# Norms of q and kv and the key rotation moved into the input projection, the convolution norms' steps listed per engine, the dilated up map ahead of the sparse one

## The reference

```
z = modulate(rmsnorm(x, g_pre_mix), shift, scale) @ w_in      # 1024 -> 1696 columns
zq, ckv, k_rope, conf, sc = parts of z                        # 256, 128, 32, 512, 768
q = rmsnorm(zq, g_q) @ w_q_b; q's last 32 of 96 columns of a head are rotated
k, v = rmsnorm(ckv, g_kv) @ w_kv_b; k_rope is rotated, and shared by all 8 heads
attn = softmax(q k / sqrt(96)) v
conf = silu(layernorm(depthwise_conv(a * sigmoid(g), 31 taps)))
sc   = b * depthwise_conv(c * h, 3 taps)
y = concat(rmsnorm(attn), rmsnorm(conf), rmsnorm(sc)) @ w_o
x = x + gate * rmsnorm(y, g_post_mix); then the same around w2(relu(w1 h)^2)
```

```
merged = sigmoid(m0) * (y_nsa @ w_up_nsa) + sigmoid(m1) * (y_dil @ w_up_dil)
x = x + merged @ w_o;  x = x + peer(rms_norm(x))      # product-key experts
```

## Time and profile before

| what | us |
|---|---|
| median of 3 runs | 4206.3 (4204.83 to 4207.1) |
| profiled execution | 4206.12 |
| its span | 4204.8 |
| PE busy | 3946.2 (94%) |
| PEld busy | 3112.9 (74%) |
| DVE busy | 2139.9 (51%) |
| ACT busy | 1520.0 (36%) |
| POOL busy | 495.0 (12%) |

### The profile page before, as it was taken

One profiled execution on the slowest core, in us unless ns is written; L12 is line 12 of the kernel. 1 busy time (PEld: TensorE's weight loads), 2 busy tenths in 40 slices (PEclk: granted clock), 3 DMA queues, 4 the chain that ended last, 5 costly groups with the idle time before them and its releaser, 6 DMA issues.

```text
span 4204.8 us, 47670 instructions
## 1 busy us (share of the span) xinstructions
PE 3946.2 (94%) x19722; PEld 3112.9 (74%) x19722; DVE 2139.9 (51%) x3752; ACT 1520.0 (36%) x1876; POOL 495.0 (12%) x748
## 2 busy tenths in 40 slices
PE   6988989999898889998899989999998999999999
PEld 4845768888774468885787877878887788888887
DVE  2165343333446444444544445788873566654444
ACT  3245442212235542225554423344443322222222
POOL 0000000000000000000001000267556111100000
PEclk8999999999999999999999999999999999999999
DMA  5400122332110022222214232354545666543332
GB/s 189 164 18 1 61 78 104 120 111 100 51 70 13 1 80 90 90 100 95 74 38 127 82 119 92 137 169 156 169 153 186 189 193 187 180 150 116 110 126 85
DMA packets 109832, 459.76 MB, mean 109 GB/s; under 512 B 9216, under 2 KB 43120, under 8 KB 68912
## 3 DMA queue, kind: packets, MB, share of 16 engines
q1 hardware_dynamic: 82048, 354.96, 24.3%
q0 software_dynamic: 27568, 101.74, 8.1%
HBM read 389.04 MB, written 67.63 MB: 109 GB/s over the span
## 4 chain that ended last, share of the span: by engine, by line
PE 81%; DVE 8%; ACT 5%; POOL 2%; DMA 2%; issue 1%; SPq 0%; DVEq 0%; ACTq 0%; POOLq 0%
PE ps L554 22%; PE ps L556 22%; PE ps L555 22%; PE ps L2323 2%; PE ps L981 2%; PE ps L634 1%; DVE ACC L1194 1%; POOL Y L2459 1%; PE ps L476 1%; DVE MX L1167 1%; PE ps L1061 1%; PE ps L1870 1%; DVE TD L711 1%; DMA gdram<-GST 1%; PE ps L1889 1%
## 5 line engine op out<-in xcount | busy, mean ns | idle before, releaser
L554 PE MATMUL ps<-HH,WH 128*128 128x512 f32 x2760 | 1058.1, 383 | 54.1 <-DVE HL L675 36.5
L555 PE MATMUL ps<-HL,WH 128*128 128x512 f32 x2760 | 1048.8, 380 | 0.0
L556 PE MATMUL ps<-HH,WL 128*128 128x512 f32 x2760 | 1048.8, 380 | 0.0
L447 DVE TENSOR_TENSOR WL<-stage,WH 128x2048 fp32r<-128x2048 f32 x248 | 567.3, 2287 | 483.6 <-ACT WH L436 483.6
L436 ACT ACTIVATE WH<-stage 128x2048 fp32r<-128x2048 f32 x248 | 472.8, 1907 | 585.8 <-PE ps L556 539.6
L554 PEld LDWEIGHTS ps<-HH,WH 128*128 128x128 f32 x2760 | 523.7, 190 | 167.1 <-issue 51.0
L556 PEld LDWEIGHTS ps<-HH,WL 128*128 128x128 f32 x2760 | 524.8, 190 | 105.7
L555 PEld LDWEIGHTS ps<-HL,WH 128*128 128x128 f32 x2760 | 523.7, 190 | 102.6 <-issue 0.5
L554 PE MATMUL ps<-AHp,WH 128*128 128x512 f32 x1024 | 406.9, 397 | 7.1 <-ACT Y L2641 7.1
L555 PE MATMUL ps<-ALp,WH 128*128 128x512 f32 x1024 | 406.5, 397 | 0.0
L556 PE MATMUL ps<-AHp,WL 128*128 128x512 f32 x1024 | 406.4, 397 | 0.0
(11 more groups left out here) (366 smaller groups left out, 4955.3 us busy)
## 6 DMA issues: line engine op xcount, KB each, us to landing
stage<-in_w SPq DMA_DIRECT2D x64, 1024.0 KB, 4.8
stage<-in_u SPq DMA_DIRECT2D x64, 1024.0 KB, 4.9
stage<-in_v SPq DMA_DIRECT2D x64, 1024.0 KB, 4.9
stage<-in_w_mod SPq DMA_DIRECT2D x48, 1024.0 KB, 4.9
GR<-gdram POOLq DMA_DIRECT2D x32, 1024.0 KB, 7.9
adram<-GR SPq DMA_DIRECT2D x22, 1024.0 KB, 3.9
AR<-adram POOLq DMA_DIRECT2D x88, 256.0 KB, 3.5
gdram<-GST SPq DMA_DIRECT2D x16, 1024.0 KB, 5.8
```

The lines of the kernel that those rows point to most:

```text
L447: dve.e.tensor_tensor(k.WL[o % 2][:, 0:w], k.stage[n % 2][:, 0:w], k.WH[o % 2][:, 0:w].bitcast(F32), ALU.subtract).then_inc(*dve.done("sla ...
L554: pe.e.matmul(o, wh[:, kk, cs], L.hh[:, kk, z], start=first, stop=False)
L555: pe.e.matmul(o, wh[:, kk, cs], L.hl[:, kk, z], start=False, stop=False)
L556: mm = pe.e.matmul(o, wl[:, kk, cs], L.hh[:, kk, z], start=False, stop=last)
```

## The change

In w_in, ScalarE squares kv and q after chunk q1, into three rows of Y instead of TA (the ring ZS). After chunk g1 TensorE sums them, and ScalarE does both Ln and then both Exp. After chunk a1 TensorE rotates the key, and DVE scales kv and q and finishes the rope. WKV moves to the place of the TD buffers, outside of what w_in's inputs occupy, and is loaded as soon as the key is rotated; the ropes of q inside attention get scratch of their own (TDa). WQ's load stays where it was. V's six products and copies become entries of `att_order`, between the three parts of head 0.

`att_behind` names the sum ("stat"), the root, the scaling ("normed", "centered") and the SiLU as separate entries; both products of a sum stand together; the PSUM tile of a sum is held until the entry of its root; the taps of the short convolution are spread between them. The sums of a pair of heads go into Y's own rows.

In the merge the dilated map comes first, in the plan of slabs too, and the three DVE steps go to the sparse chunks. w_o2 waits for each low part by itself and pairs its first two chunks.

```diff
     k.ta = [new(f"TA{i}", [128, 768]) for i in range(2)]
+    k.WKV = nc.alloc_sbuf_tensor_at("WKV", [128, 1024], F32, offset=base.at)
     k.td = [new(f"TD{i}", [128, 768]) for i in range(2)]
...
     k.WQ = new("WQ", [128, 2, 768])
-    k.WKV = new("WKV", [128, 1024])
+    k.tda = [new(f"TDa{i}", [96, 512]) for i in range(2)]
...
         plain(("dvs", hp), 1, lambda s: io[f"dvs{hp}"])
     plain("wmg", 8, lambda s: io["wmg"][s])
+    plain("up_dil", 1, lambda s: io["up_dil"])
     plain("up_nsa", 2, lambda s: io["up_nsa"][s])
-    plain("up_dil", 1, lambda s: io["up_dil"])
     plain("w_o2", 4, lambda s: io["w_o2"][s])
     plain("wq2", 4, lambda s: io["wq2"][s])
     for g in range(32):
...
-def tensor_stat(k, pe, name, c, n, segs, ring=None):
-    ring = ring or k.psum
+def tensor_stat(k, pe, name, c, n, segs, ring=None, squares=None, keep=False):
+    ring, squares = ring or k.psum, squares or k.TA
     if c == 0:
...
 def tensor_z(k, pe, l):
+    segs = both(l)
     for c in tensor_linear(k, pe, z_linear(k, l)):
-        pass
+        if c == 6:
+            tensor_stat(k, pe, ("kvn", l), 0, 1, [LAT, CTX], None, k.ZS)
+            for j in range(2):
+                tensor_stat(k, pe, ("qn", l), j, 2, segs, None, k.ZS)
+        if c == 7:
+            p = k.psum.take(pe, ("krot", l), ("rope_s", (l, "k")))
+            pe.wait_ge("z_act", (l, "kr"))
+            pe.wait_ge("rotM", 0)
+            pe.e.matmul(p[0:96, 0:512], k.rotM[:, :], k.KR[:, 0:512], start=True, stop=True).then_inc(*pe.done("rot", (l, "k")))
 def scalar_z(k, act, l):
...
         i.then_inc(*act.done("z_act", (l, kind)))
+        if kind == "q1":
+            act.wait_ge("z_act", (l, "q1"))
+            scalar_square(k, act, ("kvn", l), 0, k.ZKV, 0, 768, k.ZS)
+            for j in range(2):
+                scalar_square(k, act, ("qn", l), j, k.ZQ[:, j, :], a, b, k.ZS)
+        if kind == "g1":
+            rows = [(("kvn", l), 128, [LAT, CTX], ("kv_normed", l)), (("qn", l), 256, both(l), ("q_normed", l))]
+            for name, D, segs, end in rows:
+                scalar_rstd_log(k, act, name, 1 if D == 128 else 2, D, segs, k.psum, end)
+            for name, D, segs, end in rows:
+                scalar_rstd_root(k, act, name, segs)
 def vector_z(k, dve, l):
...
         i.then_inc(*dve.done("z_dve", (l, kind)))
+        if kind == "a1":
+            col, segs = k.cols[l], both(l)
+            vector_norm_in_place(k, dve, ("kvn", l), [k.ZKV[:, :]], [LAT, CTX], lambda c: col[:, G_KV + c:G_KV + c + 1],
+                                 ("kv_normed", l))
+            vector_norm_in_place(k, dve, ("qn", l), [k.ZQ[:, j, :] for j in range(2)], segs,
+                                 lambda c: col[:, G_Q + c:G_Q + c + 1], ("q_normed", l))
+            vector_rope(k, dve, k.KR, ("krot", l), (l, "k"))
...
 def att_behind(l):
-    out = []
+    out, short = [], []
     for j in range(2):
         out += [("tap", 0, j, t) for t in range(31)] + [("conv", 4 + j)]
     for j in range(2):
-        out += [("tap", 1, j, t) for t in range(3)] + [("conv", 6 + j)]
-    out += [("center",), ("sq", "conf", 0), ("sq", "conf", 1), ("silu",)]
-    out += [("sq", "br4", 0), ("sq", "br4", 1), ("branch", 4)]
-    return out + [("sq", "br6", 0), ("sq", "br6", 1), ("branch", 6)]
+        short += [("tap", 1, j, t) for t in range(3)] + [("conv", 6 + j)]
+    out += [("center",)] + short[0:2] + [("centered",)] + short[2:4] + [("sq", "conf", 0), ("sq", "conf", 1)]
+    out += short[4:6] + [("stat", "conf")] + short[6:8] + [("root", "conf"), ("sq", "br6", 0), ("sq", "br6", 1)]
+    out += [("normed",), ("stat", "br6"), (None,), ("silu",), ("root", "br6"), ("sq", "br4", 0), ("sq", "br4", 1)]
+    return out + [("branch", 6), ("stat", "br4"), (None,), ("root", "br4"), (None,), ("branch", 4)]
 def att_order(l):
...
     scored, turned, outs, pairs, head, done = [], [], [], [], [], 0
-    for part in range(3):
-        yield "head", (0, part)
+    yield "head", (0, 0)
+    for tt in range(4):
+        yield "v", tt
+    yield "head", (0, 1)
+    yield "v", 4
+    yield "v", 5
+    yield "head", (0, 2)
     for n, u in enumerate(units + [None, None, None]):
         ended = pairs.pop(0) if pairs else None
         if outs:
...
 def tensor_att(k, pe, l):
     segs = both(l)
     if l == 0:
         tensor_mod_close(k, pe, 0, 21)
     for kind, u in att_order(l):
         if kind == "head":
             tensor_head(k, pe, l, *u)
+        elif kind == "v":
+            p = k.psum.take(pe, ("v", l, u), ("v", (l, u)))
+            pe.wait_ge("kv_normed", l)
+            pe.wait_ge(f"wkv{l}", 0)
+            pe.e.matmul(p[:, 0:512], k.ZKV[:, 128 * u:128 * u + 128],
+                        k.WKV[:, :].rearrange("p (h a d) -> p h a d", h=8, a=2)[:, :, 1, :],
+                        start=True, stop=True).then_inc(*pe.done("v_mm", (l, u)))
         elif kind == "scores":
             h, q0, k0, kn = u
             p = k.psum.take(pe, ("s", l, u), ("p_exp", (l, u)))
...
+        elif u[0] == "stat":
+            for j in range(2):
+                tensor_stat(k, pe, (u[1], l), j, 2, segs, keep=True)
+        elif u[0] == "root":
+            k.psum.give(("stat", (u[1], l)), ("rstd_ln", (u[1], l)))
     pe.mark(f"att{l}")
...
     act.wait_ge(*z_linear(k, l).end)
     for kind, u in att_order(l):
+        if kind == "v":
+            act.wait_ge("v_mm", (l, u))
+            act.e.activation(k.V[:, u, :], k.psum.of(("v", l, u))[:, 0:512], ACT.Copy).then_inc(*act.done("v", (l, u)))
+        elif kind == "head":
             h, part = u
             end = ("scores", (l, (h, att_last(l)) + ((512, 256) if l == 0 else (0, 768))))
...
         elif kind == "pair":
-            t = k.TA.take(act, ("sums", l, u), ("o_scaled", (l, u)))
             act.wait_ge("turned_sums", (l, u))
-            act.e.activation(t[:, a:b], k.psum.of(("sums", l, u))[:, a:b], ACT.Copy).then_inc(*act.done("sum_rows", (l, u)))
+            act.e.activation(k.Y[:, u, a:b], k.psum.of(("sums", l, u))[:, a:b], ACT.Copy).then_inc(*act.done("sum_rows", (l, u)))
         elif kind == "att_sq":
             act.wait_ge("o_scaled", (l, u))
             scalar_square(k, act, ("att", l), u, k.Y[:, u, :], a, b)
...
             scalar_square(k, act, (u[1], l), u[2], k.Y[:, c0 + u[2], :], a, b)
+        elif u[0] == "root":
+            end = ("conf_normed", (l, 1)) if u[1] == "conf" else ("branch", (l, int(u[1][2])))
+            scalar_rstd(k, act, (u[1], l), 2, 256, segs, k.psum, end)
...
 def vector_rope(k, dve, buf, place, key):
-    t = k.TD.take(dve, ("rope", key), ("roped", key))
+    t = (k.TD if key[1] == "k" else k.TDa).take(dve, ("rope", key), ("roped", key))
     dve.wait_ge("rot", key)
     dve.e.tensor_tensor(t[0:96, 0:512], k.psum.of(place)[0:96, 0:512], k.sinM[:, :], ALU.mult).then_inc(
         *dve.done("rope_s", key))
 def pool_att(k, pool, io, l):
+    pool.wait_ge("roped", (l, "k"))
+    pool.e.dma_start(k.WKV[:, :], io["w_kv_b"][l]).then_inc(*pool.landed(f"wkv{l}"))
     pool.wait_ge(*z_linear(k, l).end)
     pool.wait_ge("norm_lo", (("x", l), 7))
     pool.e.dma_start(k.WQ[:, :, :], io["w_q_b"][l]).then_inc(*pool.landed(f"wq{l}"))
-    pool.e.dma_start(k.WKV[:, :], io["w_kv_b"][l]).then_inc(*pool.landed(f"wkv{l}"))
...
 def nsa_up_linear(k):
-    return Linear("up_nsa", 2, 4, 512, [LAT], k.YH, k.YL, lambda kk: ("y_lo", kk), lambda c: [("upn", c)], True)
+    return Linear("up_nsa", 2, 4, 512, [LAT], k.YH, k.YL, lambda kk: ("y_lo", kk), lambda c: [("upn", c)])
 def dil_up_linear(k):
     return Linear("up_dil", 1, 2, 1024, [LAT], k.YH[:, 4:6, :], k.YL[:, 4:6, :], lambda kk: ("y_lo", 4 + kk),
-                  lambda c: [("upd", c)])
+                  lambda c: [("upd", c)], True)
 def o2_linear(k):
-    return Linear("w_o2", 4, 8, 256, [LAT], k.HH2, k.HL2, lambda kk: ("um_lo", 7), lambda c: [("xo", c)])
+    return Linear("w_o2", 4, 8, 256, [LAT], k.HH2, k.HL2, lambda kk: ("um_lo", kk), lambda c: [("xo", c)], True)
...
     pool.wait_end("dil", "pe", "act", "dve")
     for c in range(16):
         if c >= 4:
-            pool.wait_ge("upn" if c < 12 else "upm", (c - 4) % 8)
+            pool.wait_ge("upd" if c < 12 else "upm", (c - 4) % 8)
         pool.wait_ge(f"ob{c % 2}", ("mg", 14 + c % 2))
-        pool.e.dma_start(k.gin[c % 4][:, :], io["mgd"][c]).then_inc(*pool.landed(f"gi{c % 4}", c))
+        pool.e.dma_start(k.gin[c % 4][:, :], io["mgd"][(c + 8) % 16]).then_inc(*pool.landed(f"gi{c % 4}", c))
 def tensor_merge(k, pe):
+    for c in tensor_linear(k, pe, dil_up_linear(k), k.psn):
+        pass
     for c in tensor_linear(k, pe, nsa_up_linear(k), k.psn):
-        pass
-    for c in tensor_linear(k, pe, dil_up_linear(k), k.psn):
         pass
     for c in tensor_linear(k, pe, o2_linear(k), k.psn):
         pass
...
     act.wait_end("dil", "pe", "dve")
     act.wait_ge("ob0", ("mg", 14))
     act.wait_ge("ob1", ("mg", 15))
-    for c in range(6):
+    for c in (4, 5, 0, 1, 2, 3):
```

(19 more changed lines are left out.)

63 lines of the change are left out of this document (16 added, 47 removed).

## The result

The changed kernel takes 4176.3 us (median of four runs, 4172.9 to 4180.5) against 4206.7 for the kernel before: a ratio of 0.9929, 95% interval 0.9912 to 0.9946. That is 0.7% faster, by 30.4 us, and by 33.2 in the two profiled executions (4206.1 and 4172.9). The forecast was 4156, 49.7 faster; its range, 4139 to 4177, held the median with 0.7 us to spare. That the range held is in part luck: nothing in the sum or in the rivals stood for the wait that ate the gain of the norms.

What follows compares the result with a forecast made beforehand. TensorE, with 81% of the chain of waits, bounds the kernel; time is saved only at its idle or low clock. 10.6 + 9.0 + 12.4 + 7.2 + 10.5 = 49.7 off 4206.1 gives 4156.4, range 4139 to 4177.

Steps and rivals of the forecast that it cites:

- Start of attention, layer 0: Last w_in product to first scores: 14.1 us instead of 31.2, less 5.0 of sums and 1.5 of wait in w_in; net 10.6.
- Start, layer 1: Last w_in product to first scores in layer 1: 13.1 us gained, 4.1 added in w_in, net 9.0 (6 to 11).
- No drain behind a table load: ScalarE's Exp load priced at 1.28 us, without the skill's drain of about 1.38, which would make the forecast 2.8 us later.
- Norms: Convolution branch norms beside attention: less TensorE idle and low clock, gaining 12.4 us in layer 0 and 7.2 in layer 1.
- idle plus clock reckoning: Loss in the norms' stretches as TensorE idle plus clock deficit times busy time: 25.9 us in layer 0, 18.7 in layer 1.
- the walk down the list: Layer 0's norm entries taken unit by unit: 9.5 us idle at roots and SiLU plus 4 for the clock, 13.5 left.
- The stalls of the roots: TensorE idle in layer 0's norms: about 1 us at the conf root, 5.5 where SiLU and br6's root meet, 3 at br4's.
- Merge: Ahead of w_o2: the 8.24 us wait goes whole, plus 2.1 from its first matmuls at low clock; 10.5 (6 to 12).
- A: Rival: the norms gain nothing since ScalarE's blocks are all still there; 30.1 us gained, 4176; chance 0.12.
- B: Rival: the norms' stalls and low clock go nearly whole, 4 us left per layer; 66.7 gained, 4139; chance 0.15.
- C: Rival, slower: sums and wait inside w_in leave TensorE at 1.2 GHz through the rest of w_in; 4256; chance 0.03.
- D: Rival: WQ lands at 7 us or more in both layers, query product at low clock; 6 us lost per layer, 4168; chance 0.08.

Runs made afterwards that it cites:

- yardstick: The changed kernel run again with nothing altered, beside the kernel before: 4177.2 us, ratio 0.9929.

## Why the prediction was right and where it failed

- **Start of attention, layer 0 (10.6).** Right in its terms: last w_in product to scores 14.2 (14.1), paid in w_in 6.6 (5.0 + 1.5), net 10.6. WQ landed 5.9 us behind its issue (5.7). That the net agrees to a tenth is luck of the trace: the yardstick's profile has 17.1 in place of 14.2, so 7.7 net.
- **Start, layer 1 (9.0).** 13.6 - 4.0 = 9.7. Putting both starts back cost 21.5 (19.6).
- **No drain behind a table load.** The load of 1.28 us at 137.83 has its Ln at 139.12. The Trainium skill's extra 1.38 (ScalarE: Activation LUTs, section What ACT_TABLE_LOAD costs) would by an estimate have made the stall in w_in 4.5 us; it was 1.78.
- **Norms (12.4 + 7.2): the step that failed.** By the same idle plus clock reckoning as the forecast's, the stretches it looked at came out at 11.8 + 0.09 x 48.2 = 16.1 us of loss in layer 0 (13.5 forecast, 25.9 before) and 5.7 + 0.05 x 30.3 = 7.2 in layer 1 (11.5 forecast, 18.7 before): a gain of 9.8 + 11.5 = 21.3 against 19.6. So much was nearly right. What was missing is a term that the walk down the list never stopped at. It counted the statistics that are held in PSUM, and it passed over the mean, whose two steps the change had also set a unit apart, without holding the tile. That cost 5.5 us in layer 0 and some 8 in layer 1, at places outside the stretches of the earlier trace rows that I had chosen for the norms. 21.3 - 13.6 = 7.7, and 6.1 were measured. Two kernels that only take this wait away gave 12.2 and 14.4 us. By the runs the term of 19.6 came out at a gain of -1.8.
- **The stalls of the roots.** Idle in layer 0: 1.5 at the conf root (about 1 forecast), 3.2 behind SiLU (5.5), 1.5 + 2.0 at br4's root (3). The clock cost 4.3 (4).
- **Merge (10.5).** The wait went whole, and w_o2's slow first products with it. 9.1 in the trace, 8.0 in a second pair; the new wait for the gate block is 0.66 of it. By the runs 6.6; whether the 2 to 3 us between come back in the expert layer is not shown.
- **Rivals.** A (the norms gain nothing) is what the runs show of the list: putting it back changes -1.8 us. Its reason, ScalarE's blocks, is not what ate the gain: they cost 19 us under the new list too, but the list had gained 10 to 13 by its order, and the mean's tile lost them again. B did not come. C did not: w_in stayed at 1.00. D came by half, in layer 0 alone. The prediction had called a query product that waits for WQ a sign of being wrong, and its own sum has no such wait as a cost beyond 1.1 us: there were 1.36 us in one profile, and in the other 2.59 with the query product at the low clock, 3 us in all. Layer 1 had no wait for WQ in either.

With the mean's steps together the forecast of 4156 would have stood against 4163.
